# RWKV chunks of 64 tokens instead of 32 in a hybrid stream encoder

## Chip, cores and metric

One core of one Trainium2 chip. The metric is the device time of one execution in microseconds (us); a kernel's time is the median of its runs.

## The reference

Two layers (DEPTH = 2) over 288 tokens: a prompt of 256 and a sample of 32 with states of its own. A layer is a feed-forward part, a projection to three head groups, an output projection, a second feed-forward part and a gated embedding. The head groups are forgetting attention (8 heads), RWKV-7 (4 heads of 64) and retention (4 heads of 64). The change is in RWKV, whose recurrence over tokens is

```python
def step(S, inp):
    r_t, w_t, k_t, v_t, kk_t, a_t = inp
    Skk = jnp.einsum('bhvk,bhk->bhv', S, kk_t)
    S = S * w_t[:, :, None, :] - Skk[..., None] * (kk_t * a_t)[:, :, None, :] + v_t[..., None] * k_t[:, :, None, :]
    return S, jnp.einsum('bhvk,bhk->bhv', S, r_t)
S, o = lax.scan(step, S0.astype(F32), xs)
o = jnp.swapaxes(o, 0, 1)
```

The output `o` of every token and the last state `S` of prompt and sample are wanted. All of it is float32.

## The kernel before

A loop in the program runs twice, once per layer. Every engine has an instruction list written out by hand, and the lists meet at named counting semaphores. Tokens stand in three tiles, j = 0, 1, 2, of 128, 128 and 32.

The recurrence is computed in chunks of CH = 32 tokens: eight of the prompt (four in each 128-token tile) and one of the sample. Each fp32 matrix product appears in the trace as two weight loads and two matmuls. In the order of TensorE's list:

- **Matrices and masks.** For every chunk and head, products of the decayed keys, queries and kappas (L1417, L1419) give the matrices inside a chunk: `am`, and with masks `xx`, `ct`, `bt`, `dt`. VectorE copies and masks them (L991 to L1008); a block of rows of a 128-token tile is one chunk, so a chunk's matrix is a 32x32 diagonal block.
- **Level loop.** The triangular system inside a chunk is inverted by doubling: level s combines blocks of 2^s rows. `blockwise` (L1426) issues one product per head and chunk. A level has a product y for each tile (levels' masked `am` times X), ScalarE's copy of y (L659), the products for X and its transpose T, and VectorE's add (L1027). VectorE also prepares the masked `am` of the next level (L1019). There are four levels.
- **u and a products.** X times the values' part (L1426 again, 64 columns), copied by ScalarE (L664), and the products for `atT` (L1471), copied by ScalarE (L668, L669) and VectorE (L1030).
- **Loop over the chunks** (U_ORDER, sample first): `u_step` (L1522, then VectorE's add L1062), `kv_part` (L1533), `u_part` (L1544), and VectorE's new state (L1070), which the next chunk waits for. Retention work is set between the steps by the table `with_chunk`: transposes (L1485), scores (L1495), kv products (L1508), on VectorE the masks of scores (L1038) and the retention state (L1052).
- **Outputs.** For each tile and pair of heads three terms accumulate in one bank of PSUM: values (L1574), u (L1576), state (L1579). VectorE copies five pieces out (L1089). The retention outputs (L1599, L1604) follow, and then the head norms.

GpSimd issues the small transfers of states and caches, in its own list, each behind a semaphore's count (`uac`, `s_ok`, `o_ok`). Weights come through SyncE's queue.

Of the kernel before, what the change touches and what calls it, by code (L numbers as in the profile page):

```python
# [21 lines left out]
ALU = mybir.AluOpType  # L22
# [40 lines left out]
CH = 32  # L63
NCH = T // CH

# [3 lines left out]
for _name, _n in (("ident", 128), ("mean", 128), ("headsum", 128), ("headmean", 128), ("rot", 128),  # L69
                  ("cos", T), ("sin", T), ("causal", 128), ("causal4", 32), ("levels", 5 * CH),  # L70
                  ("level0T", CH), ("before", CH), ("upto", CH), ("same", CH), ("restart", 512), ("retmask", 512),
                  ("retmask_s", 128), ("dquery", 2 * T), ("dstate", 2 * T), ("dchunk", 4),
                  ("fox8", 8), ("cols", 8)):
    CONSTS[_name] = (_at, _n)
    _at += _n
# [12 lines left out]
PAIR = (0, 2, 6)  # L88
AT_BANK = (6, 7, 2, 3)
U_ORDER = (8, 0, 1, 2, 3, 4, 5, 6, 7)  # L90
# [15 lines left out]
def program(nc, wcol, wfirst, x_in, p_in, consts_in, params_in, foxl_in, kc_in, vc_in, clf_in, srwkv_in, sret_in,  # L106
            nf_in, y_out, k_out, v_out, logf_out, shift_out, rwkv_out, ret_out):
    with ExitStack() as ctx:
# [91 lines left out]
        st = X.take(11, 2, HD)  # L200
# [4 lines left out]
        ml = [M.take(4, 4, CH) for _ in range(3)]  # L205
        xt = [M.take(2, 4, CH) for _ in range(3)]
        am, yy, bt, ct, dt = ([M.take(4, CH) for _ in range(3)] for _ in range(5))
# [14 lines left out]
        assert R.at <= A.at + 3 * 256 + 3 * 16 * CH  # L222
# [13 lines left out]
        F.at = A.at + 3 * 256 + 3 * 16 * CH  # L236
# [44 lines left out]
        def mats_psum(j, rows, es=slice(0, 2)):  # L281

            m = banks[rows, PAIR[j]:PAIR[j] + 2, :][:, es, :]
            return (m[:, :, 0:2 * CH].rearrange("p e (b t) -> p e b t", b=2),
                    m[:, :, 2 * CH:6 * CH].rearrange("p e (b w t) -> p e b w t", b=2, w=2),
                    m[:, :, 6 * CH:10 * CH].rearrange("p e (b w t) -> p e b w t", b=2, w=2))

        def at_cols(q):

            return atT[:, :, 0:TP].rearrange("p b (j q t) -> p q j b t", j=2, q=4)[:, q, :, :, :]  # L290

        def at_psum(q):

            return bank[AT_BANK[q]][:, 0:4 * CH].rearrange("p (j b t) -> p j b t", j=2, b=2)

        def o_cols(q):

            return ow[:, :, 0:TP].rearrange("p b (j q t) -> p q j b t", j=2, q=4)[:, q, :, :, :]

        def chunks(j):  # L300

            return [(4 * j + q, q, slice(CH * q, CH * q + CH)) for q in range(TILES[j][1] // CH)]
# [6 lines left out]
            u_ps u_ok s_ps s_ok o_ps o_ok gn_ps gn_sq gn_ln gn_rs  # L309
# [67 lines left out]
        with nc.Fori(0, DEPTH) as layer:  # L377
            with nc.Block() as block:
# [40 lines left out]
                def _(pool):  # L419

                    pool.dma_start(st[:, 0, :, :], srwkv_in[layer, 0]).then_inc(S["mixin"], 16)  # L421
                    pool.dma_start(st[:, 9, :, :], srwkv_in[layer, 1]).then_inc(S["mixin"], 16)
# [29 lines left out]
                    pool.wait_ge(S["uac"], 6)  # L452
# [3 lines left out]
                    pool.wait_ge(S["s_ok"], 18)  # L456
                    pool.dma_start(rwkv_out[layer, 0], st[:, 8, :, :]).then_inc(S["zstore"], 16)
                    pool.dma_start(rwkv_out[layer, 1], st[:, 10, :, :]).then_inc(S["zstore"], 16)
# [4 lines left out]
                    pool.wait_ge(S["o_ok"], 5)  # L463
# [25 lines left out]
                def _(act):  # L489
# [146 lines left out]
                    act.wait_ge(S["dend"], 1)  # L636
# [12 lines left out]

                    for j in range(3):  # L650
# [4 lines left out]
                    for s in range(1, 5):  # L655
                        for j in range(3):
                            n = TILES[j][1]
                            act.wait_ge(S["y_ps"], 3 * (s - 1) + j + 1)
                            act.activation(yy[j][0:n, :, :], bank[PAIR[j]][0:n, 0:4 * CH].rearrange("p (g t) -> p g t", g=4),  # L659
                                           ACT.Copy).then_inc(S["ycp"], 1)  # L660
# [6 lines left out]
                    for q in range(2):  # L667
                        act.activation(at_cols(q), at_psum(q), ACT.Copy).then_inc(S["uac"], 1)  # L668
                    act.activation(atT[:, :, TP:T], bank[AT_BANK[0]][:, 4 * CH:6 * CH].rearrange("p (b t) -> p b t", b=2),  # L669
                                   ACT.Copy).then_inc(S["uac"], 1)  # L670
# [110 lines left out]
                def _(dve):  # L781
# [122 lines left out]
                    for b in range(2):  # L904
# [4 lines left out]
                    chunks = lc.rearrange("p b (n u) -> p (b n) u", u=CH)  # L909
                    dve.tensor_tensor(eend.rearrange("p b (n u) -> p (b n) u", u=CH),  # L910
                                      chunks[:, :, CH - 1:CH].to_broadcast([P, 2 * NCH, CH]), chunks,
# [64 lines left out]
                    def mask(name, rows, i=0):  # L976
                        n = rows.stop
                        m = c(name)[rows, CH * i:CH * i + CH]
                        return m.unsqueeze(1).unsqueeze(1).to_broadcast([n, 2, 2, CH])

                    def by_e(x, j, rows):
                        return x[j][rows, :, :].rearrange("p (e b) t -> p e b t", e=2)

                    def four(name, rows, i=0):
                        return c(name)[rows, CH * i:CH * i + CH].unsqueeze(1).to_broadcast([rows.stop, 4, CH])

                    for j in range(3):
# [3 lines left out]
                        dve.tensor_copy(by_e(am, j, rows), first).then_inc(S["amc"], 1)  # L991
                        dve.tensor_tensor(by_e(xx, j, rows), second[:, :, :, 0, :], mask("level0T", rows), ALU.mult)\
                           .then_inc(S["masks"], 1)
                        dve.tensor_tensor(by_e(ct, j, rows), second[:, :, :, 1, :], mask("upto", rows), ALU.mult)\
                           .then_inc(S["masks"], 1)
                        dve.wait_ge(S["amc"], j + 1)
                        dve.tensor_tensor(tt[j][rows, :, :], am[j][rows, :, :], four("levels", rows, 0), ALU.mult)\
                           .then_inc(S["tt0"], 1)
                        dve.tensor_tensor(ml[j][rows, 0, :, :], am[j][rows, :, :], four("levels", rows, 1), ALU.mult)\
                           .then_inc(S["lev"], 1)  # L1000
                        dve.tensor_tensor(by_e(bt, j, rows), third[:, :, :, 0, :], mask("before", rows), ALU.mult)\
                           .then_inc(S["masks"], 1)
                        dve.tensor_tensor(by_e(dt, j, rows), third[:, :, :, 1, :], mask("upto", rows), ALU.mult)\
                           .then_inc(S["masks"], 1)
# [3 lines left out]
                        dve.tensor_tensor(both, both, c("same")[rows, :].unsqueeze(1).to_broadcast([rows.stop, 8, CH]), ALU.add)\  # L1008
                           .then_inc(S["xt"], 1)
# [5 lines left out]
                    for s in range(1, 5):  # L1015
# [210 lines left out]
                def _(pe):  # L1226
# [179 lines left out]
                    for j in range(3):  # L1406
                        if j == 2:
                            pe.wait_ge(S["trc"], 6)
# [589 lines left out]
```

## Time and profile before

| what | value |
|---|---|
| median of 3 runs | 1589.57 us (1584.37 to 1590.63) |
| the profiled execution | 1587.49 us |
| its span in the trace | 1585.9 us |
| mean granted clock of TensorE | 0.912 |
| busy share: TensorE, VectorE, ScalarE, GpSimd | 95%, 49%, 37%, 13% |
| from the first matrix product to the last retention output, layer 0 and layer 1 | 72.4 us, 73.9 us |

Busy shares are means over the span. The granted clock is the share of TensorE's full clock that the throttle let through: 1.00 is 2.4 GHz, 0.50 is 1.2 GHz. The span is a little shorter than the execution's time, since it runs from the first to the last recorded instruction. The last line is from stage windows of the trace; the RWKV part and the retention work set between it take about 146 us of the program.

### The profile page before, as it was taken

What the parts mean: (1) busy time and instruction counts of PE and PEld (TensorE: products, weight loads), DVE (VectorE), ACT (ScalarE), POOL (GpSimd) and SP (SyncE); (2) the same over time, 40 slices, a digit from 0 to 9 for tenths busy, and PEclk for the clock granted to TensorE, in tenths of its full rate; (3) what the DMA queues carried; (4) which work ended last, traced back from release to release, by engine and by line L of the source; (5) the groups of instructions that cost most, each with busy time, mean ns of one, the idle gap of its engine ahead of it and who ended that gap; (6) DMA issues with size and microseconds to landing.
All of it is one profiled execution on the core that took longest, in us unless ns stands there. A gap on an engine that the chain in (4) does not pass through costs nothing. (4 is left out here: it accounts for less than half of the span.)

```text
span 1585.9 us, 30891 instructions
## 1 busy us (share of the span) xinstructions
PE 1499.9 (95%) x13100; PEld 1399.6 (88%) x13100; DVE 782.0 (49%) x1140; ACT 592.8 (37%) x875; POOL 199.9 (13%) x129
## 2 busy tenths in 40 slices
PE   7999999987989999999989999998979999999997
PEld 6999989987756899999889999898876488999997
DVE  4555334663354355553565553447524543555535
ACT  4433334532033544332444442445211334444333
POOL 1000016751110000000000000177402000000000
PEclk9999999996586999999989999999856679999999
DMA  7444433431012244444344444243301022444443
GB/s 291 171 159 160 162 130 132 160 127 44 22 47 80 107 157 161 159 161 166 129 142 171 169 160 159 107 159 134 137 7 68 3 83 104 169 172 160 160 166 133
DMA packets 32047, 209.64 MB, mean 132 GB/s; under 512 B 4392, under 2 KB 6072, under 8 KB 7752
## 3 DMA queue, kind: packets, MB, share of 16 engines
q1 hardware_dynamic: 29392, 200.01, 34.8%
q0 software_dynamic: 2560, 8.26, 1.5%
q8 instruction: 72, 1.18, 0.3%
q14 instruction: 23, 0.19, 0.0%
HBM read 204.16 MB, written 4.10 MB: 131 GB/s over the span
## 5 line engine op out<-in xcount | busy, mean ns | idle before, releaser
L802 DVE TENSOR_TENSOR split_w<-wc,split_w 128x2048 fp32r<-128x2048 f32 x140 | 320.5, 2292 | 375.2 <-ACT split_w L529 375.2
L529 ACT ACTIVATE split_w<-wc 128x2048 fp32r<-128x2048 f32 x140 | 268.3, 1916 | 541.1 <-PE bank L1268 342.1
L1262 PE MATMUL bank<-split_x,split_w 128*128 128x288 f32 x2816 | 398.9, 299 | 15.4 <-ACT split_x L535 15.4
L1262 PEld LDWEIGHTS bank<-split_x,split_w 128*128 128x128 f32 x2816 | 386.4, 191 | 19.9 <-ACT split_w L529 13.3
L1285 PE MATMUL bank<-split_x,split_w 128*128 (+1 forms) x2112 | 282.2, 295 | 0.0
L1285 PEld LDWEIGHTS bank<-split_x,split_w 128*128 128x128 f32 x2112 | 281.8, 188 | 0.0
L1268 PE MATMUL bank<-split_x,split_w 128*128 128x288 f32 x1408 | 202.2, 296 | 0.1
L1268 PEld LDWEIGHTS bank<-split_x,split_w 128*128 128x128 f32 x1408 | 192.6, 189 | 0.3 <-DVE split_w L802 0.3
L429 POOL TENSOR_TENSOR split_x<-wc,split_x 128x1024 fp32r<-128x1024 f32 x32 | 80.1, 2503 | 499.1 <-ACT split_x L573 499.0
L573 ACT ACTIVATE split_x<-wc 128x1024 fp32r<-128x1024 f32 x62 | 65.6, 1060 | 117.9 <-PE bank L1339 117.8
L1336 PE MATMUL bank<-split_h,split_x 128*128 128x288 f32 x496 | 84.5, 312 | 7.6 <-ACT split_h L578 7.4
L1336 PEld LDWEIGHTS bank<-split_h,split_x 128*128 128x128 f32 x496 | 73.8, 197 | 12.6 <-issue 9.0
L429 POOL TENSOR_TENSOR split_e<-wc,split_x 128x1024 fp32r<-128x1024 f32 x30 | 78.5, 2618 | 17.6 <-ACT split_x L573 17.6
L1336 PE MATMUL bank<-split_x 128*128 128x288 f32 x496 | 80.2, 306 | 0.0
L1336 PEld LDWEIGHTS bank<-split_x 128*128 128x128 f32 x496 | 73.1, 196 | 0.7
L828 DVE SCALAR_TENSOR_TENSOR et<-et,bank 128x288 f32<-128x288 f32 x88 | 40.0, 455 | 45.8 <-PE bank L1268 45.8
L1756 PE MATMUL bank<-split_x,split_w 128*128 128x288 f32 x384 | 52.9, 297 | 0.0
L1756 PEld LDWEIGHTS bank<-split_x,split_w 128*128 128x128 f32 x384 | 51.7, 189 | 1.1 <-ACT split_x L767 1.1
L1426 PE MATMUL bank<-arena 32*32 32x32 f32 (+1 forms) x1728 | 36.9, 243 | 13.0 <-issue 11.9
L1426 PEld LDWEIGHTS bank<-arena 32*32 32x32 f32 x1728 | 34.6, 147 | 14.8 <-issue 14.8
L421 POOL DMA_DIRECT2D extra<-srwkv_in x2 | 1.3, 658 | 355.9 <-issue 345.5
L1339 PE MATMUL bank<-split_h,split_x 128*128 128x288 f32 x256 | 41.1, 305 | 0.0
(283 smaller groups left out, 1522.4 us busy)
## 6 DMA issues: line engine op xcount, KB each, us to landing
wc<-wcol SPq DMA_DIRECT2D x174, 1024.0 KB, 4.7
wc<-wfirst SPq DMA_DIRECT2D x12, 1024.0 KB, 4.8
arena<-kc_in POOLq DMA_DIRECT2D x8, 256.0 KB, 3.4
arena<-vc_in POOLq DMA_DIRECT2D x2, 1024.0 KB, 5.0
con<-consts_in SPq DMA_DIRECT2D x1, 1862.0 KB
xT<-x_in SPq DMA_DIRECT2D x2, 576.0 KB, 4.2
k_out<-zT POOLq DMA_DIRECT2D x8, 144.0 KB, 2.5
v_out<-zT POOLq DMA_DIRECT2D x8, 144.0 KB, 2.6
```

Of the source, the lines that this page charges most:

```text
L429: pool.tensor_tensor(lo, z_raw(n), hi, ALU.subtract).then_inc(S["zlo"], 1)
L529: act.activation(ws[s % 2][0], wc[:, p % RING, :], ACT.Copy).then_inc(S["cast"], 1)
L573: act.activation(zw[n % 2][0], z_raw(n), ACT.Copy).then_inc(S["zcast"], 1)
L802: dve.tensor_tensor(lo, wc[:, (POS_FFN[f] + s) % RING, :], hi, ALU.subtract).then_inc(S["wlo"], 1)
L828: dve.scalar_tensor_tensor(e, e, 0.5, bank[2 * (q % 4) + 1][:, 0:T], ALU.mult, ALU.mult)\
L1262: pe.matmul(o, hi[:, k, cs], x[:, k, :], start=(w == 0 and k == 0), stop=False)
L1268: mm = pe.matmul(o, lo[:, k, cs], h_hi[:, k, :], start=False, stop=(k == DB - 1))
L1285: return pe.matmul(bank[m][:, 0:T], w[:, kk, m * 128:m * 128 + 128], rhs, start=start, stop=stop)
L1336: pe.matmul(o, hi[:, k, :], x[:, k, :], start=(w == 0 and k == 0), stop=False)
L1339: mm = pe.matmul(o, lo[:, k, :], zh_hi[:, k, :], start=False, stop=(k == DB - 1))
L1426: mm = pe.matmul(out(rows, g), left[j][rows, g, :], right(rows, g), start=True, stop=True)
L1756: mm = pe.matmul(bank[2 * s + cc][:, 0:T], w[:, k, cc * 128:cc * 128 + 128], x[:, k, :], start=(n == 0 and k == 0), stop=(n == 2 and k == ...
```

## The change

Chunks have 64 tokens: two in each 128-token tile, and the sample's 32 stay one chunk (`CHUNKS`). Diagonal blocks of the prompt are 64x64, those of the sample 32x32. The prompt needs five levels, the sample four (`LAST_LEVEL`). The loop over the chunks has the sample with chunk 0 and three more steps; the retention work is spread anew over them. The masked `am` of the levels has two buffers that take turns, so preparing one waits for the y product that read the other. `yy` shares the memory of `bt`. ScalarE copies `am` for the two large tiles. In the outputs the state term is no longer accumulated with the other two: it is a group of products of its own, into a bank of its own; ScalarE copies the first part, and VectorE adds the second to it. Constants grow by 352 columns. Counts that GpSimd waits for follow the new numbers.

```diff
-CH = 32
-NCH = T // CH
+CH = 64
+CHUNKS = ((0, 0, 0, 64), (0, 64, 64, 64), (1, 0, 128, 64), (1, 64, 192, 64), (2, 0, 256, 32))
+SAMPLE = 4
+LAST_LEVEL = (5, 5, 4)
...
-PAIR = (0, 2, 6)
-AT_BANK = (6, 7, 2, 3)
-U_ORDER = (8, 0, 1, 2, 3, 4, 5, 6, 7)
+LEVEL_AT = (2, 6, 0)
+AT_BANK = (6, 7)
+U_ORDER = (SAMPLE, 0, 1, 2, 3)
...
+                    for j in range(2):
+                        act.wait_ge(S["mats_ps"], j + 1)
+                        act.activation(am[j].rearrange("p (e b) t -> p e b t", e=2), mats_psum(j, slice(0, P))[0],
+                                       ACT.Copy).then_inc(S["amc"], 1)
...
+                    act.wait_ge(S["o_ps"], 1)
+                    for r in range(2):
+                        act.activation(by_half(ow, r), halves_psum(r), ACT.Copy).then_inc(S["o_half"], 1)
+                    act.activation(ow[:, :, TP:T], sample_psum(0, 256), ACT.Copy).then_inc(S["o_half"], 1)
...
-                    for s in range(1, 5):
-                        if s < 4:
-                            for j in range(3):
+                    for s in range(1, 6):
+                        for j in range(3):
+                            if s < LAST_LEVEL[j]:
                                 rows = slice(0, TILES[j][1])
-                                dve.tensor_tensor(ml[j][rows, s, :, :], am[j][rows, :, :], four("levels", rows, s + 1),
-                                                  ALU.mult).then_inc(S["lev"], 1)
+                                if s > 1:
+                                    dve.wait_ge(S["y_ps"], 3 * (s - 2) + j + 1)
+                                dve.tensor_tensor(ml[j][rows, (s + 1) % 2, :, :], am[j][rows, :, :],
+                                                  mask("levels", j, 4, s + 1), ALU.mult).then_inc(S["lev"], 1)
...
-                    with_chunk = {2: [(ret_scores, 0)], 4: [(ret_scores, 1)], 6: [(ret_scores, 2)],
-                                  7: [(ret_state, i) for i in range(5)]}
+                    with_chunk = {1: [(ret_scores, 0)], 2: [(ret_scores, 1)],
+                                  3: [(ret_scores, 2)] + [(ret_state, i) for i in range(5)]}
...
+                    dve.wait_ge(S["o_half"], 3)
+                    dve.wait_ge(S["o_ps"], 2)
+                    for r in range(2):
+                        dve.tensor_tensor(by_half(ow, r), by_half(ow, r), halves_psum(2, 256 * r), ALU.add)\
+                           .then_inc(S["o_ok"], 1)
...
-                    with_chunk = {1: [(ret_tok, 0), (ret_scores, 0)], 2: [(ret_tok, 1)], 3: [(ret_scores, 1)],
-                                  4: [(ret_tok, 2)], 5: [(ret_scores, 2)], 6: [(ret_kv, i) for i in range(5)]}
-                    u_step(8)
+                    with_chunk = {0: [(ret_tok, 0), (ret_scores, 0)], 1: [(ret_tok, 1), (ret_scores, 1)],
+                                  2: [(ret_tok, 2), (ret_scores, 2)], 3: [(ret_kv, i) for i in range(5)]}
+                    u_step(SAMPLE)
...
-                            for ch, q, rows, e, g, hs in each:
-                                mm = pe.matmul(o_of(q, hs), st[hs, ch if ch < 8 else 9, b, :],
-                                               ar[hs, b, 1, CH * ch:CH * ch + CH], start=False, stop=True)
+                    mm.then_inc(S["o_ps"], 1)
+                    for i, (j, r, t0, n) in enumerate(CHUNKS):
+                        for b in range(2):
+                            for e in range(2):
+                                hs = slice(64 * e, 64 * e + 64)
+                                o = bank[2][:, 4 * r + 128 * j + 64 * b:4 * r + 128 * j + 64 * b + 64] if i != SAMPLE \
+                                    else bank[3][:, TS * b:TS * b + TS]
+                                mm = pe.matmul(o[hs, :], st[hs, of_chunk(i)[3], b, :], ar[hs, b, 1, t0:t0 + n],
+                                               start=True, stop=True)
                     mm.then_inc(S["o_ps"], 1)
```

## Rows read from the trace of the kernel before

**Rows 1.** The page: busy us, share of the span, instructions.

```profile
PE 1499.9 (95%) x13100; PEld 1399.6 (88%) x13100; DVE 782.0 (49%) x1140; ACT 592.8 (37%) x875; POOL 199.9 (13%) x129
```

**Rows 2.** Stage windows, layer 0: us, engines' busy time, clock, DMA share, GB/s.

```profile
359.31:366.07 6.76, 4.31 (x290) 3.90 (x290) 5.53 (x25) 0.97 (x3) 3.57 (x7) 0.98 0.48 171
366.07:388.25 22.18, 16.10 (x811) 15.12 (x810) 7.52 (x23) 4.08 (x15) 0.00 (x0) 0.50 0.02 4
388.25:393.23 4.98, 4.28 (x130) 4.00 (x130) 0.49 (x2) 1.70 (x6) 0.28 (x1) 0.50 0.01 3
393.23:417.03 23.80, 23.00 (x292) 17.92 (x292) 9.69 (x34) 1.78 (x3) 0.81 (x2) 0.50 0.03 8
417.03:425.28 8.25, 8.25 (x217) 7.49 (x217) 2.13 (x10) 0.00 (x0) 2.16 (x4) 0.50 0.10 36
425.28:431.68 6.40, 6.40 (x67) 4.35 (x65) 2.70 (x9) 0.00 (x0) 0.00 (x0) 0.50 0.00 0
```

**Rows 3.** Stage windows, layer 1, matrices and masks, level loop.

```profile
1140.46:1148.04 7.58, 4.44 (x288) 4.03 (x288) 5.72 (x25) 0.97 (x3) 3.58 (x7) 0.96 0.43 153
1148.04:1170.95 22.91, 15.98 (x810) 15.14 (x809) 7.39 (x23) 3.96 (x15) 0.00 (x0) 0.50 0.02 4
```

**Rows 4.** TensorE's timeline, level loop: start, us, engine, line, instructions, idle before.

```profile
374.44 2.25 PE L1426 MATMUL bank<-arena 32*32 32x32 f32 x128 [0.74 <-issue]
377.89 2.44 PE L1426 MATMUL bank<-arena 32*32 32x32 f32 x126 [1.21 <-issue]
381.42 2.50 PE L1426 MATMUL bank<-arena 32*32 32x32 f32 x128 [1.08 <-issue]
```

**Rows 5.** Windows of one microsecond, level loop.

```profile
382.00:383.00 1.00, 1.00 (x66) 1.00 (x55) 0.57 (x2) 0.00 (x0) 0.00 (x0) 0.50 0.06 16
```

**Rows 6.** The page: queue of the instruction transfers, packets, MB, share.

```profile
q8 instruction: 72, 1.18, 0.3%
```

**Rows 7.** Waits of the weight loads, 359 to 432: us, times, longest.

```profile
PEld bank L1426 <- issue: 7.1, 7, 1.4
```

**Rows 8.** TensorE's timeline, short windows in one form each.

```profile
376.08 0.61 PE L1426 MATMUL bank<-arena 32*32 32x32 f32 x8
...
395.13 1.06 PE L1544 MATMUL bank<-arena,extra 32*64 32x64 f32 x16
...
413.06 1.19 PE L1508 MATMUL bank<-arena 64*64 64x64 f32 x32
```

**Rows 9.** VectorE's timeline, matrices and masks.

```profile
360.54 0.29 DVE L991 COPY arena<-bank 128x128 f32<-128x128 f32 x1 [5.00 <-PE bank L1419]
...
361.74 0.28 DVE L1003 TENSOR_TENSOR arena<-bank,con 128x128 f32<-128x128 f32 x1
361.94 0.41 DVE L1008 TENSOR_TENSOR arena<-arena,con 128x256 f32<-128x256 f32 x1
362.27 0.28 DVE L991 COPY arena<-bank 128x128 f32<-128x128 f32 x1
...
365.76 0.74 DVE L1013 TENSOR_TENSOR hT<-zT,con 128x576 f32<-128x576 f32 x1
```

**Rows 10.** Timeline of TensorE and its weight loads, loop over the chunks.

```profile
396.58 0.64 PE L1522 MATMUL bank<-extra,arena 64*32 64x64 f32 x8 [0.38 <-DVE extra L1070]
397.14 0.50 PEld L1533 LDWEIGHTS bank<-extra 32*64 32x64 f32 x8 [0.17 <-issue]
398.35 0.69 PE L1485 MATMUL bank<-con,hT 128*128 128x128 f32 x2
...
413.06 1.80 PE L1508 MATMUL bank<-arena 64*64 64x64 f32 x40
414.79 0.64 PE L1522 MATMUL bank<-extra,arena 64*32 64x64 f32 x8
```

**Rows 11.** TensorE's timeline, outputs, tile 0.

```profile
417.03 0.47 PE L1574 MATMUL bank<-arena,extra 32*64 32x32 f32 x16 [0.39 <-DVE extra L1070]
...
418.64 0.46 PE L1574 MATMUL bank<-arena,extra 32*64 32x32 f32 x16
```

More of the change, by code:

```diff
@@ L204, in program @@
         u0 = M.take(3, 256)
-        ml = [M.take(4, 4, CH) for _ in range(3)]
-        xt = [M.take(2, 4, CH) for _ in range(3)]
-        am, yy, bt, ct, dt = ([M.take(4, CH) for _ in range(3)] for _ in range(5))
+        wide = (CH, CH, TS)
+        ml = [M.take(2, 4, w) for w in wide]
+        am = [M.take(4, w) for w in wide]
+        xt = [M.take(2, 4, w) for w in wide]
+        bt, ct, dt = ([M.take(4, w) for w in wide] for _ in range(3))
+        yy = bt
         xx, tt = zip(*((x[:, 0, :, :], x[:, 1, :, :]) for x in xt))
@@ L973, in _, with mask, mask_e, by_e @@
                         link(dve.tensor_tensor(qk, qk, rott[:], ALU.add))
[L976 to L985, printed above, removed]
+                    def mask(name, j, k, i=0):
+                        n, w = TILES[j][1], wide[j]
+                        m = c(name)[0:n, CH * i:CH * i + w]
+                        return m.unsqueeze(1).to_broadcast([n, k, w])
+                    def mask_e(name, j):
+                        n, w = TILES[j][1], wide[j]
+                        return c(name)[0:n, 0:w].unsqueeze(1).unsqueeze(1).to_broadcast([n, 2, 2, w])
+                    def by_e(x, j):
+                        return x[j][0:TILES[j][1], :, :].rearrange("p (e b) t -> p e b t", e=2)
                     for j in range(3):
@@ L1007, in _ @@
                         both = xt[j][rows, :, :, :].rearrange("p x g t -> p (x g) t")
-                        dve.tensor_tensor(both, both, c("same")[rows, :].unsqueeze(1).to_broadcast([rows.stop, 8, CH]), ALU.add)\
-                           .then_inc(S["xt"], 1)
+                        dve.tensor_tensor(both, both, mask("same", j, 8), ALU.add).then_inc(S["xt"], 1)
                     dq, ds_ = (c(x).rearrange("p (b t) -> p b t", b=2) for x in ("dquery", "dstate"))
@@ L1028, in _ @@
-                    dve.wait_ge(S["at_ps"], 2)
-                    for q in range(2, 4):
-                        dve.tensor_copy(at_cols(q), at_psum(q)).then_inc(S["atc"], 1)
+                            if s <= LAST_LEVEL[j]:
+                                rows, w = slice(0, TILES[j][1]), wide[j]
+                                k = 8 if s < LAST_LEVEL[j] else 4
+                                d = bank[LEVEL_AT[j] + 1][rows, 0:k * w]
+                                both = xt[j][rows, :, :, :].rearrange("p x g t -> p (x g t)")[:, 0:k * w]
+                                dve.wait_ge(S["dx_ps"], 3 * (s - 1) + j + 1)
+                                dve.tensor_tensor(both, both, d, ALU.add).then_inc(S["lvl"], 1)
@@ L1424, in blockwise @@
                         for g in range(4):
-                            for ch, q, rows in chunks(j):
+                            for ch, rows, ts_ in chunks(j):
                                 mm = pe.matmul(out(rows, g), left[j][rows, g, :], right(rows, g), start=True, stop=True)
@@ new lines, in _ @@
+                            at, w = 128 * j + wide[j] * b, wide[j]
+                            each = [(rows, e, 2 * e + b, slice(64 * e, 64 * e + 64))
+                                    for ch, rows, ts_ in chunks(j) for e in range(2)]
+                            for rows, e, g, hs in each:
+                                pe.matmul(bank[rows.start // 64][hs, at:at + w], tok[rows, j, 6 + b, hs], dt[j][rows, g, :],
+                                          start=True, stop=False)
+                            for rows, e, g, hs in each:
+                                mm = pe.matmul(bank[rows.start // 64][hs, at:at + w], u0[rows, j, HD * g:HD * g + HD],
+                                               ct[j][rows, g, :], start=False, stop=True)
@@ L1815, in constants @@
     lv = []
-    for s in range(5):
+    for s in range(6):
         w = 1 << s
```

253 lines of the change are left out of this document (123 added, 130 removed).

## The prediction

> **What bounds the kernel now.** I began with the share of busy time on the page. TensorE's matmuls have 95% of the span, its weight loads, which overlap them, 88%, VectorE 49% [rows 1]. That is a mean over the program, and the change touches only the RWKV part, so the next view is the busy time by stage. I cut layer 0 where the kind of work changes: matrices and masks (6.76 us), level loop (22.18), u and a products (4.98), loop over the chunks (23.80), outputs (8.25), retention outputs (6.40) [rows 2]. Together 72.4 us. Layer 1 repeats them, but for the first two, which take 7.58 and 22.91 [rows 3]. What the reader is to see: the granted clock is 0.50 (1.2 GHz) from the level loop on, and in the loop over the chunks and the outputs TensorE is busy for nearly the whole stage, while in the level loop it is busy for only 16.10 of 22.18 us.
>
> So the level loop has another bound, and the timeline of TensorE tells which. Its matmuls come in lots of 126 to 128, and the lots begin 3.45 and 3.53 us apart, each behind a gap that no semaphore explains [rows 4]. In such a stretch the DMA moves 16 GB/s for one microsecond, 16 KB, and in the next nothing [rows 5]; the page has an instruction queue of 72 packets and 1.18 MB, 16.4 KB a packet [rows 6]. The chain of waits charges 7.1 us in seven idle times of the weight loads to "issue" [rows 7]. I read it so: TensorE's instructions arrive in blocks of 128 matmuls with their weight loads, and a block takes about 3.45 us. The level loop's 792 matmul records (11 sets of products, 72 records each) make 6.2 blocks, 21.4 us, against 22.18 measured. The loop is paced by its number of instructions, not by their size.
>
> How long the array needs for a product comes from neighbours in one form [rows 8]. A single 32x32 tile: eight records in 0.61 us; a lone one of that shape shows about 0.24, so (0.61 - 0.24)/7 = 53 ns apart. Two 64-wide tiles taking turns: sixteen in 1.06 us, in pairs (1.06 - 0.31)/7 = 107 ns apart, hence two records per 107 ns. Four 64x64 tiles: 32 in 1.19 us, about four per 107 ns.
>
> **The change part by part**, each stage as new minus old.
>
> *Matrices and masks.* VectorE sets the end here in layer 0: its first mask operation starts 1.23 us into the stage, and 128x128 operations follow at 0.20 us, 128x256 ones at 0.33 [rows 2, 9]. A 64-token tile has masks of 256 columns: six at 0.33 (the copy goes to ScalarE) and the add over 512 columns, about 0.6 by the 0.74 of the 576-column row, make 2.6 us where there were 1.73. Two tiles, then five operations of the sample at 0.20, put the sample's last mask at 1.23 + 5.2 + 1.0 + 0.07 = 7.5 us. Behind it stands the sample's product with the values, eight records of one tile at 107 ns (0.86) and a change of form (0.17, below): the first level product starts at 8.6 us, against 6.76 and 7.58. That is +1.8 and +1.0 us. The smaller number of matrix records also hides the fetch gap of this stage.
>
> *Level loop.* The groups of four heads on a 128-token tile are now 8 products, 16 records on two 64x64 tiles: 8 x 107 ns = 0.86 us for y, twice that, 1.71, for X and its transpose. The sample keeps single 32x32 tiles, 8 records at 53 ns: 0.43 and 0.86. A level is 2 x 0.86 + 0.43 + 2 x 1.71 + 0.86 = 6.43 us, plus four changes between the forms. The trace shows such a change in the chunk step: the weight loads of the next form come 0.17 us late [rows 10]. So 7.11 us for each of three levels, 6.68 for the fourth (the sample's transpose is left out), 3.44 for the fifth (no sample, no transpose): 31.5 us. Fetching no longer counts: 536 records are 4.2 blocks, 14.4 us. ScalarE's copies (256 columns, about 0.41 by VectorE's row) and VectorE's adds (512 columns, below the 0.74 of 576) each fall beneath another tile's products of 0.86 us or more [rows 9]; uncovered, a level would add about 1.2 us. The balance is +9.3 in layer 0 and +8.5 in layer 1.
>
> *u and a products.* Three u groups of 0.86, a products of 0.86 (four tiles) and 0.43, two form changes and 0.7 of copies with their waits, as before: 4.9 us against 4.98; with the larger copy (256 columns for 128) I take +0.1.
>
> *Loop over the chunks.* One step takes 398.35 - 396.58 = 1.77 us. The old stage is 3.35 for sample and first chunk, seven steps (12.39), 0.80 in which TensorE idles, and the remainder, 7.26, retention work set between the steps; the trace shows its longest piece, 1.73 us for the kv products [rows 2, 10]. A step with 64 rows has the same number of products with the same 64 columns, so the same 1.77, and there are three instead of seven. Sample and first chunk now differ in form, say +0.3. The retention work is only moved. 3.65 + 5.31 + 7.26 + 0.80 = 17.0 us: -6.8. The idle time stays in the sum because the scores of the second and third tile must now wait for VectorE in the same step (about 0.2 us each). GpSimd issues the loads of the retention state behind the same copies as before, and VectorE wants them in the last step only, some 13 us later.
>
> *Outputs.* Old: the three terms of one 128-token tile and one pair of heads take 418.64 - 417.03 = 1.61 us [rows 11]. New: the first two terms on four tiles, 64 records at four per 107 ns, 1.7 us; the sample 1.0; the state products as groups of their own, 32 records in pairs, 1.7, and the sample 0.6; with a quarter of slack 5.25 us against 8.25: -3.0. ScalarE's copies and VectorE's adds of the two parts run beneath the 6.40 us of retention outputs, in which VectorE has 2.70 and ScalarE nothing to do [rows 2]; without that cover they would cost about 1.5 us. Larger constants at the start and GpSimd's changed wait counts I set at nothing, taking the longer transfer to be hidden behind those of the first weights. Without that cover the 180 KB more (352 columns of 128 rows of 4 bytes) cost 1.1 us at the 171 GB/s of the first stage [rows 2].
>
> *Sum.* Layer 0: 1.8 + 9.3 + 0.1 - 6.8 - 3.0 = +1.4. Layer 1: 1.0 + 8.5 + 0.1 - 6.8 - 3.0 = -0.2. Together +1.2 on the profiled execution's 1587.49, 1588.7; that execution lies 2.1 below the median of the runs shown, so 1590.8 there: **1591 us**. Bounds: some 25 form changes a layer at nothing instead of 0.17 give -8.5; at twice that +8.5. If the four-tile groups run only as pairs, the a products and outputs cost 2.6 more a layer, +5.2.
>
> **Rivals.** *The level loop gets its clock.* A loop without fetch gaps keeps TensorE busy without a break, and the clock might go to 2.4 GHz after the first level. Then, at half the pitch and the same form changes, 7.11 becomes 3.8 twice, 6.68 becomes 3.6, 3.44 becomes 1.7, which is 11.4 us a layer, 22.8 in all: 1568 us. Against it: the retention outputs are busy for 6.40 of 6.40 us and the chunk loop for 23.00 of 23.80, on tiles of this size, all at 0.50 [rows 2]. The Trainium skill, "TensorE: Matmul & The Clock Gate", Part 1, What's actually happening, says that the default is the throttled state and that activity releases it; by that rule alone this rival would be the forecast and the sum 1568. The stage rows do not agree with it as it stands, for being busy did not release the clock there. Chance 0.13.
>
> *The form change costs more.* This is the slower side. The row with 0.17 us stands between groups whose next records were already at hand. In the level loop, 64x64 and 32x32 products alternate four times a level, and if each change waits for the records before it to finish, it costs about 0.31 + 0.05 us, a lone record's length and a start. It decides from about 0.30 us on: 50 changes in two layers at 0.13 more are 6.7 us, which carries 1590.8 past 1597.5; at 0.4 us it is 1602. For it: the sample's short groups leave little to overlap. Against it: the chunk step has three such changes and its 1.77 us hold no more than 0.17 for one [rows 10]. The Trainium skill, "TensorEngine Tiling (Array Packing)", Tiling Modes, Key Properties, says that changing the mode, not just the tile, drains TensorE; it gives no price, so nothing follows from it but the sign. Chance 0.15.
>
> *The change does nothing to the pacing*, that is, fetching still sets the level loop: 14.4 us of blocks, about 17 us less a layer than my sum, 1557. It needs products of 64 columns to cost no more than those of 32, and the pitches of 53 and 107 ns speak against it [rows 8]. Chance 0.02.
>
> **How the numbers follow.** The forecast's case has 0.70, with a range of its own from 1582 to 1600, from the bounds above. About 8 us, 0.5%, is what a measurement of this kernel can tell from no change. Of the 0.70, 0.03 lie below 1581.6, 0.04 above 1597.5, 0.63 between. With the rivals: faster 0.03 + 0.13 + 0.02 = 0.18; slower 0.04 + 0.15 = 0.19; same 0.63. To hold 8 in 10 the range takes in the lower part of the slower rival and leaves out the two fast ones: 1580 to 1602.
>
> **What would show it.** Right: level loop near 31 us at clock 0.50 with no lots of 128 and hardly an "issue" gap, groups of sixteen 64x64 records 0.86 us apart; chunk loop near 17 us; outputs near 5; first level product 8 to 9 us after the first matrix product. Wrong: a granted clock of 1.00 inside the levels; gaps of 0.3 us or more at each sample group; a level longer than 7.5 us with waits on VectorE's adds or ScalarE's copies; or retention outputs that start late because the outputs' two parts are added too late.

## The result

The new kernel takes 1566.94 us (median of 4 runs, 1566.34 to 1569.28) against 1590.1 of the kernel before (4 runs); the ratio is 0.9856, 95% interval 0.9817 to 0.9895. Measured once more with six runs it was 1567.46 (1547.85 to 1569.35), ratio 0.9818 (0.9776 to 0.9860). The forecast was 1591 with a range from 1580 to 1602: wrong. The first rival, the level loop with its clock, had 1568.

The stage windows of the new kernel, layer 0, answer to [rows 2]: matrices and masks, level loop, u and a products, loop over the chunks, outputs, retention outputs. Columns as there; the clock is the last but two.

```profile
359.26:368.16 8.90, 5.47 (x162) 4.71 (x161) 7.39 (x23) 1.74 (x5) 3.55 (x7) 0.86 0.36 128
368.16:388.50 20.34, 20.31 (x537) 19.17 (x537) 11.41 (x26) 5.71 (x17) 0.00 (x0) 0.89 0.01 3
388.50:391.95 3.45, 2.75 (x81) 2.39 (x81) 0.84 (x2) 1.64 (x5) 0.00 (x0) 1.00 0.02 5
391.95:407.84 15.89, 15.50 (x197) 12.03 (x197) 6.06 (x21) 1.78 (x3) 1.84 (x4) 0.53 0.04 10
407.84:413.02 5.18, 5.18 (x123) 4.93 (x121) 2.28 (x10) 0.78 (x3) 1.39 (x3) 0.50 0.13 51
413.02:419.42 6.40, 6.40 (x67) 4.35 (x65) 2.57 (x7) 0.00 (x0) 0.00 (x0) 0.50 0.01 3
```

Layer 1 answers to [rows 3] with these two, and is alike in the rest (60.23 us in all against 60.16):

```profile
1133.71:1142.61 8.90, 5.47 (x161) 4.71 (x161) 7.39 (x23) 1.74 (x5) 3.56 (x7) 0.88 0.36 128
1142.61:1163.13 20.52, 20.48 (x538) 19.36 (x537) 11.41 (x26) 5.71 (x17) 0.00 (x0) 0.88 0.01 3
```

What the reader is to see is the clock of the level loop, 0.89 where all of the RWKV part had 0.50, and that TensorE is busy for 20.31 of its 20.34 us. Cut by levels, the loop shows when the clock rose: the first 4.35 us at 1.2 GHz, the rest at 2.4 GHz. The rows of the second and third level have 4.07 us each. The last row is the loop over the chunks after its first microsecond: the clock has gone down again.

```profile
368.16:372.51 4.35, 4.35 (x77) 4.17 (x78) 1.90 (x5) 1.94 (x6) 0.00 (x0) 0.50 0.01 4
372.51:374.44 1.93, 1.93 (x62) 1.82 (x60) 1.54 (x3) 0.00 (x0) 0.00 (x0) 1.00 0.00 0
374.44:378.51 4.07, 4.07 (x128) 3.85 (x126) 2.58 (x7) 1.00 (x3) 0.00 (x0) 1.00 0.01 4
378.51:382.58 4.07, 4.07 (x128) 3.85 (x126) 2.58 (x7) 1.00 (x3) 0.00 (x0) 1.00 0.01 4
...
393.00:407.80 14.80, 14.41 (x176) 11.16 (x172) 5.55 (x20) 1.78 (x3) 0.99 (x3) 0.50 0.04 11
```

The waits of the weight loads in that loop, which were 7.1 us of "issue" in [rows 7], are down to a single one of 0.2 us, and the instruction queue moves 62 packets in place of the 72 of [rows 6]. The stage rows of a layer count 1807 matmul records before and 1167 after: 640 fewer, five lots of 128 a layer, ten in two layers, as many as the packets that are gone:

```profile
PEld bank L1450 <- issue: 0.2, 1, 0.2
```

```profile
q8 instruction: 62, 1.02, 0.3%
```

Stage by stage, in us, layer 0 / layer 1. The level loop and the u and a products stand together, because the first u product of the old kernel belongs to a lot that began before the boundary that I had drawn.

| stage | before | predicted | measured |
|---|---|---|---|
| matrices and masks | 6.76 / 7.58 | 8.6 / 8.6 | 8.90 / 8.90 |
| level loop, u and a products | 27.16 / 27.89 | 36.6 / 36.5 | 23.79 / 23.96 |
| loop over the chunks | 23.80 / 23.81 | 17.0 | 15.89 / 15.79 |
| outputs | 8.25 / 8.24 | 5.25 | 5.18 / 5.19 |
| retention outputs | 6.40 / 6.40 | 6.40 | 6.40 / 6.39 |
| sum | 72.37 / 73.92 | 73.9 / 73.8 | 60.16 / 60.23 |

The stages gain 12.2 + 13.7 = 25.9 us; the profiled spans differ by 1585.9 - 1565.4 = 20.5. The remaining 5.4 are given back in work that the change does not touch: from the head norms of layer 0 to its second feed-forward part, that part, and layer 1 up to its matrices take 114.85, 251.57 and 342.36 us before, and 118.03, 252.53 and 343.73 after, that is +3.2, +1.0 and +1.4. Their clocks are lower by 0.03, 0.01 and less than 0.01. The rows of the first (before, then after):

```profile
431.68:546.53 114.85, 105.54 (x560) 76.03 (x559) 55.19 (x119) 44.34 (x100) 8.62 (x11) 0.81 0.20 74
```

```profile
419.42:537.45 118.03, 108.60 (x560) 77.25 (x559) 55.30 (x119) 44.34 (x100) 8.59 (x11) 0.78 0.20 72
```

### The profile page after: what moved, and what is told of

The parts are those of the page before. It is cut to its first block and busy times, and to the rows that moved or that the text cites. A ratio compares the mean times of both kernels' runs of the same rounds, so it can differ in the third digit from the quotient of the medians.

```text
span 1565.4 us, 28327 instructions
## 1 busy us (share of the span) xinstructions
PE 1492.4 (95%) x11820; PEld 1393.6 (89%) x11820; DVE 791.6 (51%) x1116; ACT 598.7 (38%) x887; POOL 199.6 (13%) x129
## 5 line engine op out<-in xcount | busy, mean ns | idle before, releaser
L1359 PEld LDWEIGHTS bank<-split_h,split_x 128*128 128x128 f32 x496 | 74.7, 198 | 12.2 <-issue 9.0
L1450 PE MATMUL bank<-arena 64*64 64x64 f32 (+2 forms) x1152 | 44.3, 228 | 0.2
L1450 PEld LDWEIGHTS bank<-arena 64*64 64x64 f32 (+1 forms) x1152 | 41.5, 141 | 3.1 <-issue 0.7
```

Source lines behind the costliest of these rows:

```text
L1359: pe.matmul(o, hi[:, k, :], x[:, k, :], start=(w == 0 and k == 0), stop=False)
L1450: mm = pe.matmul(out(rows, g), left[j][rows, g, :], right(rows, g), start=True, stop=True)
```

## The experiments

The first theory was **no breaks**: the new level loop gets 2.4 GHz because TensorE streams there without a break, and the old one had breaks because it waited for its instructions. Its rival was **size of the products**: that 64x64 tiles, not the missing breaks, raise the clock. The first kernel below keeps the 64x64 products and puts breaks in; the second keeps 32x32 products and closes the breaks, but only by making each product longer.

**Breaks put into the new loop.** ScalarE copies the first tile's y five times in every level, each behind the one before.

```diff
                                 act.wait_ge(S["y_ps"], 3 * (s - 1) + j + 1)
+                                for i in range(4 if j == 0 else 0):
+                                    act.activation(yy[j][0:n, :, :].rearrange("p g t -> p (g t)"),
+                                                   bank[LEVEL_AT[j]][0:n, 0:4 * w], ACT.Copy).then_inc(S["pad"], 1)
+                                    act.wait_ge(S["pad"], 4 * (s - 1) + i + 1)
```

> The new kernel, but ScalarE makes its copy of the first tile's y product five times in a row in every level, each behind the one before, so that TensorE has a break of about 1 us (1.2 GHz) to 1.5 us (2.4 GHz) in each of the five levels. Nothing else changes. Theory 'no breaks' (the clock rises in the new level loop because TensorE streams there without a break): the granted clock stays 0.50 in the whole loop, which takes 31.5 us by the prediction's sum plus five breaks of about 1, some 36 us instead of 20.4; the kernel comes to about 1595. Theory 'size of the products' (64x64 products raise it, breaks or not): the clock goes to 1.00 as before, the loop takes 20.4 + 5 x 1.5 = 28 us, the kernel about 1582.

Measured: 1595.33 us (one run). The windows are the whole level loop, and its first part:

```profile
368.83:402.43 33.60, 27.94 (x538) 26.37 (x538) 11.49 (x26) 12.44 (x37) 0.00 (x0) 0.65 0.01 2
368.83:383.60 14.77, 13.30 (x226) 12.50 (x226) 5.25 (x12) 5.57 (x17) 0.00 (x0) 0.50 0.01 2
```

The same 64x64 products, with 5.7 us of breaks, stay at 0.50 for nearly two levels where the new kernel had its full clock after 4.35 us; later the clock goes up and down between both levels, which I had not expected, and has a mean of 0.65. The loop is 13.3 us longer, of which the breaks themselves are 5.7. So size alone does not hold the clock, and breaks hinder it without shutting it out: it also rose while they went on. The row of the first part also gives what the new loop costs at 1.2 GHz: 13.30 us of work for 226 matmuls, so 7.06 for a level's 120. The prediction had 7.11.

**The old loop with twice the columns.** In the kernel before, each 32x32 product of the level loop takes two heads' columns as its right side.

```diff
                     def cols(b, g):
-                        return bank[b][:, CH * g:CH * g + CH]
+                        return bank[b][:, 2 * CH * g:2 * CH * g + 2 * CH]
+
+                    def two(x, j, rows, g):
+                        return x[j][rows, g // 2 * 2:g // 2 * 2 + 2, :].rearrange("p g t -> p (g t)")
...
-                                      lambda rows, g: xx[j][rows, g, :]).then_inc(S["y_ps"], 1)
+                                      lambda rows, g: two(xx, j, rows, g)).then_inc(S["y_ps"], 1)
```

> The kernel before, but each 32x32 product of the level loop takes two neighbouring heads as its right side (64 columns instead of 32, the second half is not used), so the number of instructions is the same and each streams twice as long. By the prediction's pitches four such tiles take 128 records in 3.4 us at 1.2 GHz, just as long as a block of 128 takes to arrive. Theory 'paced by fetching' for the old loop: it stays at 22 to 23.5 us in spite of twice the columns. If the old loop was bound by the products' own time instead, it goes to 35 us or more. For the clock: theory 'no breaks' expects it to rise to 1.00 somewhere in the loop, since the gaps between the lots close; theory 'size of the products' (64x64 wanted) expects 0.50 throughout.

Measured: 1590.24 us (one run), the level loop of layer 0, its part at the low clock and its part at the full one, then three lots of the full clock in the timeline:

```profile
367.88:389.85 21.97, 18.43 (x796) 17.96 (x795) 7.04 (x22) 4.19 (x15) 0.00 (x0) 0.85 0.02 4
367.88:374.37 6.49, 6.49 (x208) 6.49 (x206) 2.15 (x7) 1.72 (x6) 0.00 (x0) 0.50 0.02 5
374.37:389.85 15.48, 11.94 (x591) 11.47 (x590) 4.89 (x16) 2.47 (x9) 0.00 (x0) 1.00 0.02 4
```

```profile
380.17 2.53 PE L1428 MATMUL bank<-arena 32*32 32x64 f32 x126 [1.13 <-issue]
383.99 2.61 PE L1428 MATMUL bank<-arena 32*32 32x64 f32 x128 [1.29 <-issue]
387.72 2.61 PE L1428 MATMUL bank<-arena 32*32 32x64 f32 x126 [1.13 <-issue]
```

Three things are to be seen. The loop takes 21.97 us where the old one took 20.83 between the same two products, in spite of twice the columns: it was paced by its instructions and not by their work. With the gaps closed the clock rises to 1.00 although the tiles are 32x32: size is refuted. And at 1.00, with the work done in half the time, the lots of 128 and their gaps without a releaser are back, 3.73 and 3.82 us apart: at twice the clock hardly another pace.

Two things speak against "no breaks" as the whole answer. In layer 0 the clock stayed at 1.00 to the end of the loop although the breaks were back in its last three lots. And in layer 1, where the loop took 24.49 us, it fell behind such breaks and then stayed at 0.50 for some 10 us in which TensorE had no break at all:

```profile
1156.00:1166.20 10.20, 7.59 (x389) 7.10 (x388) 3.08 (x10) 0.82 (x3) 0.00 (x0) 1.00 0.01 3
1166.20:1177.18 10.98, 10.98 (x329) 10.84 (x318) 2.27 (x9) 1.64 (x6) 0.00 (x0) 0.53 0.02 4
```

So both kernels agree with breaks that keep the clock down in the old loop, the first one by breaks alone; that work without a break brings the clock up, and how soon, they do not show.

**More form changes.** The sample's X products stand between those of tiles 0 and 1 in three levels.

```diff
                         for j in range(3):
                             if s <= LAST_LEVEL[j]:
+                                if j == 1 and s < 4:
+                                    pe.wait_ge(S["ycp"], 3 * (s - 1) + 3)
+                                    x_part(2)
                                 pe.wait_ge(S["ycp"], 3 * (s - 1) + j + 1)
-                                mm = blockwise(j, lambda rows, g: cols(LEVEL_AT[j] + 1, j, g)[rows, :], tt,
-                                               lambda rows, g: yy[j][rows, g, :])
+                                if j < 2 or s >= 4:
+                                    mm = x_part(j)
```

> The new kernel, but in three levels the sample's products for X stand between those of the first and the second tile, so that each of these levels has six changes between 64x64 and 32x32 products instead of four: six more changes a layer. At 0.17 us a change the level loop gets 1.0 us longer (20.4 to 21.4 a layer) and the kernel about 2; at the 0.36 us of the slower rival 2.2 and 4.4; if a change costs nothing at 2.4 GHz, the loop keeps its 20.4.

Measured: 1546.04 us (one run), 21 less than the new kernel, which neither price explains. The level loop and the loop over the chunks of layer 0:

```profile
367.58:389.04 21.46, 21.42 (x538) 19.87 (x537) 11.38 (x26) 5.74 (x17) 0.00 (x0) 0.90 0.01 3
...
392.48:404.26 11.78, 9.71 (x196) 7.54 (x197) 5.85 (x21) 1.78 (x3) 1.15 (x3) 1.00 0.05 14
```

The loop itself is 21.46 - 20.34 = 1.12 us longer, 0.19 us for each of six changes: the price of the prediction (0.17), not that of the slower rival. But the stage behind it kept the clock at 1.00 and took 11.78 us instead of 15.89, and the outputs 2.96 and 3.93 instead of 5.18 and 6.40. Timed again, with the expectation

> The kernel with six more form changes a layer once more, timed. Its first run had 1546 with the clock at 1.00 through the loop over the chunks in both layers, though only form changes were added. If that is the new kernel's own and was luck of one run, its times scatter between 1546 and 1569; if the shift of one microsecond holds the clock each time, all lie between 1535 and 1550.

it scattered: 1560.59, 1547.49, 1574.04 and 1569.21. In the profiled one the loop over the chunks had 1.00 in layer 0 and 0.53 in layer 1. So a time of 1546 was luck in good part. But in the new kernel as it is, the clock fell at the start of this loop in all four profiled layers (two executions), and with the microsecond more in one of four. The new kernel seems to stand near an edge, where a microsecond decides whether the clock falls; so few layers do not prove it.

**The wait before the loop over the chunks, filled.** Three 128x128 products whose result is not used, where TensorE waits for copies.

```diff
+                    def fill(k, b, at):
+                        for _ in range(k):
+                            pe.matmul(bank[b][:, at:at + 128], c("ident"), c("ident"), start=True, stop=True)
...
                     mm.then_inc(S["at_ps"], 1)
+                    fill(3, 2, 256)
                     pe.wait_ge(S["uac"], 5)
```

> The new kernel, with three 128x128 fp32 products whose result is not used (0.64 us at 2.4 GHz) put where TensorE waits 0.62 us for the copies between the a products and the loop over the chunks. Theory 'the fall at 393 us comes of that wait': the clock stays 1.00 into the loop over the chunks; that loop then takes 9 to 12 us instead of 15.9, outputs 2.7 instead of 5.2, retention outputs 3.3 instead of 6.4, as far as it lasts: 1540 to 1560 us. Rival: the loop over the chunks is itself too thin, and the clock falls a little later: 1563 to 1569, no change that counts.

Measured: 1537.11 us (4 runs, 1533.26 to 1542.02), ratio to the kernel before 0.9662 (0.9625 to 0.9699). Loop over the chunks, outputs and retention outputs of layer 0 (layer 1 has the same three times):

```profile
392.63:404.41 11.78, 9.71 (x197) 7.53 (x196) 5.86 (x21) 1.78 (x3) 1.15 (x3) 1.00 0.05 14
404.41:407.37 2.96, 2.96 (x124) 2.81 (x120) 2.27 (x10) 0.78 (x3) 1.02 (x2) 1.00 0.12 44
407.37:411.30 3.93, 3.93 (x68) 2.81 (x65) 2.53 (x7) 0.00 (x0) 1.07 (x2) 1.00 0.11 38
```

Added work makes the kernel faster: 0.17 us are lost before the loop, and 8.8 won in it and behind it. The two RWKV parts together win 17.1 of the 30.0 us between the profiled spans (1565.4 and 1535.4). The rest is won in work that the edit does not touch: 8.4 us between the two RWKV parts and 5.0 behind the second, at a slightly higher clock (these two stretches of the new kernel, then of this one):

```profile
419.42:1133.71 714.29, 688.11 (x4748) 648.01 (x4746) 363.49 (x466) 285.19 (x407) 91.15 (x49) 0.94 0.39 138
1193.94:1565.44 371.50, 353.24 (x2352) 319.20 (x2350) 184.19 (x275) 139.75 (x213) 8.66 (x11) 0.92 0.36 129
411.30:1117.17 705.87, 679.96 (x4751) 641.90 (x4747) 363.15 (x467) 285.61 (x407) 90.90 (x49) 0.95 0.39 140
1168.89:1535.39 366.50, 348.25 (x2354) 316.41 (x2350) 184.05 (x276) 139.81 (x213) 8.66 (x11) 0.93 0.36 131
```

So the time of a whole kernel does not tell by itself what the clock did in the loop over the chunks; the stage rows do.

**Unused work elsewhere.** Four such products, one more than in the run before, right before the last level, the wait left open. It asks whether filling the wait matters, or only when the wait comes.

```diff
                                     pe.wait_ge(S["lvl"], 3 * (s - 2) + j + 1)
+                                if (s, j) == (5, 0):
+                                    fill(4, 2, 256)
```

> The new kernel, with four 128x128 fp32 products whose result is not used (0.85 us) right before the last level's first y product, where TensorE has no wait; the wait of 0.62 us before the loop over the chunks stays open. It tells why the run with more form changes kept its clock: theory 'filling the wait' (what held the clock in the bridge run is work in the wait itself): it falls as in the new kernel, loop over the chunks 15.9, kernel about 1568. Theory 'how much TensorE does around the wait, and when it comes' (the fall is a matter of about a microsecond): it holds, 11.8, kernel about 1540.

Measured: 1557.78 us (4 runs: 1558.64, 1556.91, 1569.23, 1552.82), ratio 0.9779 (0.9730 to 0.9829): between the two expectations. The loop over the chunks had 1.00 in layer 0, and in layer 1 the clock fell near its end:

```profile
394.86:406.64 11.78, 9.71 (x196) 7.53 (x197) 5.85 (x21) 1.78 (x3) 1.16 (x3) 1.00 0.05 14
1159.37:1172.03 12.66, 10.58 (x196) 8.31 (x196) 5.88 (x21) 1.78 (x3) 1.86 (x4) 0.91 0.05 13
...
1177.21:1183.62 6.41, 6.41 (x67) 4.35 (x65) 2.57 (x7) 0.00 (x0) 0.00 (x0) 0.50 0.01 1
```

So the wait need not be filled for the clock to stay, but a shift does not hold it each time, and the loop over the chunks can lose it by itself.

**The waits for masks, filled.** Two times seven products where TensorE waits for VectorE's masks, alone, and together with the filling before the loop. In the new kernel these waits are 1.75 and 1.68 us:

```profile
364.14 1.34 PE L1450 MATMUL bank<-extra,arena 64*64 64x64 f32 x32 [1.75 <-DVE arena L1014]
367.17 1.05 PE L1450 MATMUL bank<-extra,arena 32*32 32x64 f32 x8 [1.68 <-DVE arena L1021]
```

```diff
                     for j in range(3):
+                        if j == 0:
+                            pe.wait_ge(S["masks"], 4)
+                            pe.wait_ge(S["amc"], 1)
+                        fill((7, 0, 7)[j], 2, 384)
                         pe.wait_ge(S["masks"], (6, 8, 12)[j])
```

> The new kernel, with two times seven 128x128 fp32 products whose result is not used (1.5 us at 2.4 GHz each time) where TensorE waits 1.7 us for VectorE's masks, before the first and the third product with the values. If the clock falls at 365.7 us because of these waits, it now stays 1.00, the first levels run at full pitch, and the level loop takes 18 to 18.5 us instead of 20.4; masks 8.9 as before; the rest of the RWKV part as in the new kernel (15.9, 5.2, 6.4), unless the wait before the loop over the chunks now falls otherwise: 1560 to 1565, or near 1535 in that case. If the clock falls in spite of it, 1567.

> Both fillings together: those before the masks' products and the three products before the loop over the chunks. If each does its own, level loop 18 to 18.5 us, loop over the chunks 11.8, outputs 3.0, retention outputs 3.9: 1537 less twice 2, 1533. If the filling of the first stage does nothing: 1537.

Measured: 1546.36 us for the first alone (one run), 1549.98 for both (4 runs, 1543.04 to 1551.43; ratio 0.9707, 0.9679 to 0.9735). Level loop and loop over the chunks of the second, layer 0, then the latter in layer 1:

```profile
367.88:386.37 18.49, 18.45 (x538) 17.39 (x537) 11.83 (x27) 5.48 (x17) 0.00 (x0) 1.00 0.02 4
389.99:401.77 11.78, 9.71 (x197) 7.53 (x196) 5.86 (x21) 1.78 (x3) 1.15 (x3) 1.00 0.05 14
1154.23:1166.89 12.66, 10.58 (x197) 8.30 (x196) 5.88 (x21) 1.78 (x3) 1.86 (x4) 0.91 0.05 13
```

The level loop behaves as expected, 18.49 us at 1.00 from its start, in both kernels and layers: the clock's fall before the level loop hangs on the waits for masks. The whole misses the expected times in both. In layer 0 the clock holds, in the kernel without the filling before the loop too, but in layer 1 it falls inside the loop over the chunks in both kernels, and with it outputs and retention outputs are back at 5.18 and 6.40. That explains little of the miss: the RWKV parts with both fillings take 104.07 us and those of the bridge alone 103.30, while the spans are 13.2 apart. 9.1 of these lie between the two RWKV parts (714.99 for 705.87) and 3.6 behind the second (370.09 for 366.50), in the same work.

**The loop over the chunks filled as well.** In addition to both fillings, two products between u and kv products of the single steps and three before two of the retention scores, where TensorE waits for VectorE.

```diff
+                            fill(3, 0, 128)
                             pe.wait_ge(S["smd"], 2 * j)
...
                         u_step(i)
+                        fill(2, 2, 256)
                         kv_part(i)
```

> Both fillings of the run before, and more in the loop over the chunks: two unused 128x128 fp32 products between u and kv products of the three single steps, where TensorE then waits 0.43 us for VectorE's sum, and three before the retention scores of the second and third tile, where it waits 0.8 us for VectorE's masks. If a clock that fell inside that loop in layer 1 fell because of these waits, it now stays 1.00 in both layers: loop 11.8 to 12.3 us, outputs 3.0, retention outputs 3.9, level loop 18.5; 1525 to 1540. If the loop's narrow products are the reason, it falls in one layer or both as before: 1543 to 1552.

Measured: 1535.04 us (6 runs, 1528.11 to 1550.82), ratio 0.9649 (0.9605 to 0.9693). Loop over the chunks, outputs and retention outputs of layer 1:

```profile
1142.45:1155.16 12.71, 12.63 (x221) 10.57 (x221) 5.86 (x21) 1.78 (x3) 1.17 (x3) 1.00 0.05 13
1155.16:1158.34 3.18, 3.18 (x125) 2.99 (x121) 2.27 (x10) 0.78 (x3) 1.11 (x3) 1.00 0.12 46
1158.34:1162.27 3.93, 3.93 (x69) 2.81 (x65) 2.54 (x7) 0.00 (x0) 0.97 (x2) 1.00 0.10 38
```

The whole RWKV part is now at 1.00 in both layers of the profiled run, 50.2 and 50.4 us instead of 60.2. That does not show that the waits in the loop had made the clock fall, since the bridge alone kept 1.00 in both of its loops too. The loop pays 0.9 us for its fillings, and what is won over the simple bridge is within the scatter of the two (intervals 0.9625 to 0.9699 and 0.9605 to 0.9693). Beside it ran the new kernel itself:

> The new kernel as it is, beside the others on one chip. Its four runs lay between 1566 and 1569, in which the clock fell right before the loop over the chunks; the two kernels that only moved this wait by a microsecond scattered between 1547 and 1574. If the new kernel is as near to that edge, some of its runs now come out near 1550; if not, all lie between 1564 and 1571.

Measured: 1556.12, 1567.37, 1567.55, 1547.85, 1569.27 and 1569.35. Two of six came out lower, but the profiled one of them (1556.12) is not the case that was expected: in both layers the clock fell at the start of the loop over the chunks as before. The retention outputs of layer 1 got it back and took 4.43 us, and the work behind them 363.94 us instead of 371.50. So times scatter for other reasons than that one wait:

```profile
391.14:407.11 15.97, 15.59 (x197) 12.06 (x197) 6.05 (x21) 1.78 (x3) 1.85 (x4) 0.53 0.04 10
1165.38:1181.01 15.63, 15.24 (x196) 11.82 (x196) 6.06 (x21) 1.78 (x3) 1.87 (x4) 0.55 0.04 10
1186.19:1190.62 4.43, 4.43 (x67) 3.10 (x65) 2.53 (x7) 0.00 (x0) 0.00 (x0) 0.86 0.01 4
```

## Why the prediction was wrong

The step that failed is the one that costs the level loop: 6.43 us of products and four form changes, 7.11 a level, *all at 1.2 GHz*, and with it the 0.13 given to the rival "the level loop gets its clock". That rival's own sum was 11.4 us less a layer, 20.1 for the loop and 1568 in all; measured are 20.34 and 20.52, and 1566.94. What the runs show in place of the step: the loop has its first 4.35 us at 1.2 GHz and the rest at 2.4 GHz, where a level takes 4.07 us.

That the rival's numbers come so near is partly luck. By its own rule (half the pitch, the same form changes) 7.11 becomes 3.9 and not 3.8, and levels at 2.4 GHz took 4.07; against that the clock rose within the first level, which took 6.28 us instead of 7.11. And the RWKV parts gained 25.9 us where the rival's sum has 21.6, while 5.4 were given back elsewhere.

The argument against it was the fault: the retention outputs and the loop over the chunks are busy nearly all the time at 0.50 [rows 2], so being busy does not raise the clock. Busy time in these rows is that in which some matmul record is open, and TensorE can be busy by it and yet not raise the clock, as the old rows show, or raise it, as the new level loop does. I took one stage at 0.50 for proof that none of such products could do better. Nor were these neighbours of the level loop's form: the retention outputs alternate 128x64 products of 128 columns with 64x64 ones. And even they could, as the row of 4.43 us shows. The Trainium skill, "TensorE: Matmul & The Clock Gate", Part 1, What's actually happening, has activity release the throttle; the level loop agrees (0.50 up to 372.5, 1.00 behind it), and so do the first 14.77 us of the run with breaks in the other direction. Layer 1 of the widened old loop, with some 10 us at 0.50 without a break, does not as it stands. What sets the level loop apart from the retention outputs of [rows 2], both without idle time, no run here settles.

Point by point:

- **The old loop is paced by its instructions:** right, and shown (twice the columns, 21.97 us for 20.83, the same lots). What I did not draw from it is that such gaps may also keep the clock down, as the run with breaks has it.
- **Pitches and level at 1.2 GHz:** right (7.06 us for 7.11).
- **A form change:** 0.17 us taken, 0.19 measured at 2.4 GHz. The slower rival's 0.36 is refuted; at 1.2 GHz it would make a level 7.87 us, where the run with breaks has 7.06 of work. (The 50 changes at 0.13 that the prediction prices at 6.7 us are 6.5.)
- **Fetching no longer counts:** right, with 0.2 us of "issue" in the loop. At 2.4 GHz the margin is small: 120 matmuls in 4.07 us are 128 in 4.34, and the widened old loop got its lots every 3.6 to 4.0.
- **Masks:** +2.1 and +1.3 us measured for +1.8 and +1.0; VectorE sets that end.
- **Loop over the chunks:** -7.9 and -8.0 for -6.8. TensorE idles for 0.39 us instead of the 0.80 that I had kept, and the first microsecond still ran at 1.00.
- **Outputs:** -3.1 for -3.0; the added parts are hidden beneath the retention outputs, which stay at 6.40. What the bank of its own for the state part is worth by itself was not tried.
- **The rest of the program**, which I took as unmoved, gave back 5.4 us by its clock. That this comes of the times at which it now begins is only argued, and it does not happen each time: in the second profiled execution of the new kernel the work between and behind the two RWKV parts took 713.60 and 363.94 us, against 708.78 and 371.55 before, 2.8 less in all.

Why the clock fell right before or in the loop over the chunks stays open. The wait for the copies may be part of it: with the wait filled, and nothing else, the clock held in both profiled layers, and the four times lie between 1533 and 1542. But it was also carried into the loop with the wait left open, in both layers of the run with four products elsewhere and of the run with the masks' waits filled, so filling this wait is not shown to be what counts. And the loop itself lost the clock in others.

## What to carry to other kernels

When a change takes small gaps out of a TensorE stage that runs at the low clock, price the stage at both clocks and give the faster one a real chance; neighbours that are busy at the low clock are no proof. Where a stage at full clock ends in a short wait and much work follows, a few unused products in the wait are a cheap trial: here 0.64 us of them a layer went with 30 us less, 17 of them in the RWKV part. And time such a kernel often, and read its stages: runs of the unchanged new kernel differ by 20 us, and much of such a difference can lie in work that an edit does not touch.

## What the runs showed of the hardware

- TensorE's instructions come in lots of 128 matmuls with their loads, in the old loop at 1.2 GHz every 3.4 to 3.9 us over both layers ([rows 4] has two of them), in the widened one at 2.4 GHz every 3.6 to 4.0: the pace does not rise with the clock. The old level loop of 32x32 products was bound by it.
- The same loop over the chunks took 15.89 us at a clock of 0.53 and 11.78 at 1.00; outputs 5.18 and 2.96, retention outputs 6.40 and 3.93. The loop gains least in proportion, since TensorE is idle for 2.1 of its 11.78 us, waiting for VectorE.
- In a loop with breaks the clock can go up and down within the loop (mean 0.65 in the run with breaks, 0.72 in layer 1 of the widened old loop). Why it does is not shown.
- The clock fell to 0.50 before the new level loop where TensorE waited 1.75 and 1.68 us for masks, and stayed at 1.00 in both layers of all three kernels in which these waits were filled.
